# A conformer-style layer on one core: POOL splits the weights of the first pass, ScalarE forms scale and shift

## What is computed

```python
cs = jax.nn.silu(c)
mod = cs @ ada_w[i] + ada_b[i]
sh1, sc1, g1, sh2, sc2, g2 = [m[:, None, :] for m in jnp.split(mod, 6, axis=-1)]
h = rms_norm(x, norm1_g[i]) * (1 + sc1) + sh1
y = conformer_conv(h, ...)          # h @ w_in, GLU, causal depthwise conv of 31 taps, LayerNorm, silu, @ w_out
x = x + g1 * y
h = rms_norm(x, norm2_g[i]) * (1 + sc2) + sh2
x = x + g2 * sq_relu_mlp(h, mlp_w1[i], mlp_w2[i])
return rms_norm(x, final_g)
```

## Time and profile before

| | |
|---|---|
| median of 3 runs | 2047.59 us (2047.4 to 2048.08) |
| profiled execution | 2046.6 us, span 2044.8 us, granted clock 0.987 |
| TensorE busy | 1983.2 us (97%) |
| VectorE busy | 1073.0 us (52%) |
| ScalarE busy | 669.7 us (33%) |
| POOL busy | 322.8 us (16%) |
| first matmul of the first pass, last of its two joined chunks | 37.07 us, 149.10 us |

### The profile page before, as it was taken

How to read it: one execution, slowest core, us unless ns; L and a number is a source line. 1 busy time by engine, 2 the same in 40 slices (tenths; PEclk the granted TensorE clock), 3 DMA queues, 4 the chain that set the end, 5 groups by cost and what they waited for, 6 DMA issues and landing times.

```text
span 2044.8 us, 21628 instructions
## 1 busy us (share of the span) xinstructions
PE 1983.2 (97%) x8658; PEld 1622.4 (79%) x8658; DVE 1073.0 (52%) x1158; ACT 669.7 (33%) x715; POOL 322.8 (16%) x193
## 2 busy tenths in 40 slices
PE   6889999999999999999999999999999999999996
PEld 3668888868787888888888888888888888888885
DVE  5979999978797877233223323333332332233244
ACT  4335555444333331321231132133123213212333
POOL 3639999920000000000000000000000000000001
PEclk9999999989999999999999999999999999999998
DMA  9962222246796567222222222222222222222212
GB/s 397 399 239 95 91 103 103 83 174 236 303 407 235 211 256 293 83 102 103 90 95 103 97 88 103 103 83 102 103 87 98 103 103 82 103 103 83 101 62 82
DMA packets 46083, 300.72 MB, mean 147 GB/s; under 512 B 4704, under 2 KB 4704, under 8 KB 10976
## 3 DMA queue, kind: packets, MB, share of 16 engines
q1 hardware_dynamic: 46048, 300.29, 39.1%
HBM read 296.08 MB, written 4.19 MB: 147 GB/s over the span
## 4 chain that ended last, share of the span: by engine, by line
PE 89%; DVE 8%; ACT 1%; DMA 1%; issue 1%; SPq 0%; DVEq 0%; ACTq 0%
PE ps L396 58%; PE ps L401 29%; DVE adar L912 2%; DVE raw L912 2%; DVE wlo L929 1%; DVE hlo L918 1%; PE ps L475 1%; DMA adar<-ada 1%; PE ps L509 0%; DMA xb<-xT 0%; DVE quad L925 0%; DVE xb L1227 0%; PE ps L467 0%; ACT hhi L760 0%; ACT whi L616 0%
## 5 line engine op out<-in xcount | busy, mean ns | idle before, releaser
L396 PE MATMUL ps<-hlo,whi 128*128 128x512 f32 (+1 forms) x1792 | 653.9, 392 | 13.2 <-DVE hlo L918 13.2
L396 PE MATMUL ps<-hhi,whi 128*128 128x512 f32 (+1 forms) x1792 | 653.2, 391 | 11.1 <-ACT sig L774 4.8
L616 ACT ACTIVATE whi<-raw 128x2048 fp32r<-128x2048 f32 x176 | 336.4, 1911 | 656.2 <-PE ps L401 656.2
L401 PE MATMUL ps<-hhi,wlo 128*128 128x512 f32 (+1 forms) x1792 | 437.2, 390 | 0.0
L929 DVE TENSOR_TENSOR wlo<-raw,whi 128x2048 fp32r<-128x2048 f32 x151 | 346.0, 2291 | 120.2 <-ACT whi L616 120.2
L396 PEld LDWEIGHTS ps<-hlo,whi 128*128 128x128 f32 x1792 | 337.1, 189 | 87.6 <-issue 11.4
L396 PEld LDWEIGHTS ps<-hhi,whi 128*128 128x128 f32 x1792 | 338.3, 189 | 83.7 <-issue 7.9
L396 PE MATMUL ps<-dhi,whi 128*128 128x512 f32 x1024 | 397.0, 389 | 0.0
L396 PE MATMUL ps<-dlo,whi 128*128 128x512 f32 x1024 | 397.0, 389 | 0.0
L401 PEld LDWEIGHTS ps<-hhi,wlo 128*128 128x128 f32 x1792 | 338.0, 189 | 70.6
L1160 DVE SCALAR_TENSOR_TENSOR xb<-ps,modb,xb 128x512 f32<-128x512 f32 x128 | 90.4, 747 | 363.1 <-PE ps L401 353.3
(11 more groups left out here) (122 smaller groups left out, 828.6 us busy)
## 6 DMA issues: line engine op xcount, KB each, us to landing
raw<-w SPq DMA_DIRECT2D x176, 1024.0 KB, 4.8
raw<-ada SPq DMA_DIRECT2D x56, 1024.0 KB, 7.4
adar<-ada SPq DMA_DIRECT2D x40, 1024.0 KB, 7.2
xb<-xT SPq DMA_DIRECT2D x8, 1024.0 KB, 8.8
out<-xb SPq DMA_DIRECT2D x5, 512.0 KB, 4.2
out<-xb SPq DMA_DIRECT2D x6, 256.0 KB, 3.7
csb<-c SPq DMA_DIRECT2D x1, 1024.0 KB, 4.7
quad<-c SPq DMA_DIRECT2D x1, 1024.0 KB, 7.0
```

The source lines that it names most:

```text
L396: return pe.matmul(ps[:, bank, :], whi[:, slot, tile * P:(tile + 1) * P], x, start=first, stop=False, skip_group_check=True)
L401: return pe.matmul(ps[:, bank, :], wlo[:, slot, tile * P:(tile + 1) * P], x, start=False, stop=last, skip_group_check=True)
L616: act.activation(whi[:, q % WS, :], raw_slot(q), ACT.Copy).then_inc(whi_done, 1)
```

## The change

1. POOL splits weight units 0 to 9 in the order in which they come (before, VectorE split 0 to 8 and POOL began with 9). `raw_slot(q)` gives it the right slot.
2. POOL's 48 one-column operations and their semaphore go. VectorE multiplies the scale's bias with `norm1_g` once, for all chunks (one more small step, `small` ends one higher), and ScalarE forms scale and shift of chunk k itself, in two one-column activations ahead of `h_first(k)`.
3. VectorE does ada units 0 and 1 before it waits for the parameters.
4. VectorE's order for chunk k is: ada unit 2k + 2, `scale_x(k + 1)`, `lo_part(k)`, ada unit 2k + 3 (chunks 0 and 1 differ: 4 and 5, and none).
5. ScalarE's `split_hi((k + 1) / 2)` stands behind `h_first(k)` instead of ahead of it.
6. In the first pass TensorE does chunk 14 for all banks ahead, without waiting for the low part of chunk 15; only chunk 15 is done bank by bank.

```diff
@@ -53,7 +53,7 @@
 GLU_AT = {1: (4, 6), 2: (5, 14), 3: (6, 22), 5: (7, 3), 6: (8, 10), 7: (9, 16), 8: (10, 22), 10: (11, 8),
           11: (12, 15), 12: (13, 20)}
 FIN_POOL = 11
-SMALL_G1 = 2 * KC + 4
+SMALL_G1 = 2 * KC + 5
 
 
 PARAMS = [("ada_b", ADA), ("norm1_g", KC), ("norm2_g", KC), ("final_g", KC), ("b_in", 2 * KC), ("b_dw", KC),
@@ -419,7 +418,7 @@
                         last = low(o, s, 8 * kk + o, ch(hhi, k), False)
                 last.then_inc(unit_done, 1)
 
-            def outer_units(q, h0, order=range(8)):
+            def outer_units(q, h0, order=range(8), chunk_first=False):
                 for s in range(2):
                     outer_unit(q, s, h0)
                 with loop(ET.PE, 1, 3) as i:
@@ -427,9 +426,19 @@
                         outer_unit(q, s, h0, i)
                 outer_unit(q, 0, h0, 3)
                 pe.wait_ge(wlo_done, q + 8)
+                kks = (0, 1)
+                if chunk_first:
+                    pe.wait_ge(hhi_done, h0 + KC - 1)
+                    for o in range(8):
+                        high(o, 1, o, ch(hhi, KC - 2), False)
+                    pe.wait_ge(hlo_done, h0 + KC - 1)
+                    for o in range(8):
+                        high(o, 1, o, ch(hlo, KC - 2), False)
+                        low(o, 1, o, ch(hhi, KC - 2), False)
+                    kks = (1,)
                 pe.wait_ge(hlo_done, h0 + KC)
                 for n, o in enumerate(order):
-                    for kk in range(2):
+                    for kk in kks:
                         k = KC - 2 + kk
                         high(o, 1, 8 * kk + o, ch(hhi, k), False)
                         high(o, 1, 8 * kk + o, ch(hlo, k), False)
@@ -486,7 +495,7 @@
 
             keep_busy(14, 0, 1)
             pe.wait_ge(rstd_done, 1)
-            outer_units(A0, 0)
+            outer_units(A0, 0, chunk_first=True)
 
             for s in range(2):
                 pe.wait_ge(glu_done, s + 1)
@@ -649,9 +658,17 @@
             root(1, 7)
             preload(ACT.Sigmoid)
 
+            def scale_shift(k):
+
+                act.wait_ge(ada_used, 2 * k + 2)
+                act.activation(modb[:, 2 * k:2 * k + 1], mod[:, 2 * k:2 * k + 1], ACT.Identity,
+                               scale=col("norm1_g", k), bias=b1p[:, k:k + 1]).then_inc(small, 1)
+                act.activation(modb[:, 2 * k + 1:2 * k + 2], mod[:, 2 * k + 1:2 * k + 2], ACT.Identity,
+                               bias=col("ada_b", 2 * k + 1)).then_inc(small, 1)
+
             def h_first(k):
 
-                act.wait_ge(small, 2 * k + 4)
+                act.wait_ge(small, 2 * k + 5)
                 act.wait_ge(scaled_done, k + 1)
                 if k >= 2:
                     act.wait_ge(hlo_done, k - 1)
@@ -659,13 +676,13 @@
                                bias=modb[:, 2 * k + 1:2 * k + 2]).then_inc(hf_ready, 1)
                 h_hi(k, k, h32[k % 2])
 
-            h_first(0)
-            for k in range(1, KC):
+            act.wait_ge(par_in, 16)
+            act.wait_ge(small, 3)
+            for k in range(KC):
+                scale_shift(k)
+                h_first(k)
                 if k % 2:
                     split_hi((k + 1) // 2)
-                h_first(k)
-
-            act.wait_ge(par_in, 16)
 
             def sigmoid(c, bank, n):
 
@@ -896,10 +913,6 @@
                 dve.wait_ge(dv, steps[0])
 
             dve.memset(ones[:], 1.0).then_inc(ones_set, 1)
-            dve.wait_ge(par_in, 16)
-            dve.tensor_scalar(b1p[:, 0:KC], pr[:, COL["ada_b"]:COL["ada_b"] + 2 * KC:2], 1.0, None, ALU.add
-                              ).then_inc(small, 1)
-            dve.tensor_scalar(b1p[:, KC:2 * KC], col("ada_b", M_SC2, KC), 1.0, None, ALU.add).then_inc(small, 1)
 
             def variance(bank):
                 chain(dve.tensor_scalar(st[:, 0:4], ps[:, bank, 0:4], 1.0 / D, EPS, ALU.mult, ALU.add))
@@ -938,26 +951,31 @@
                     dve.tensor_tensor(ssum[:], ssum[:], src[:], ALU.add).then_inc(done, 1)
 
             dve.wait_ge(cs_ready, 1)
-            for a in range(3):
-                ada_reduce(a)
+            ada_reduce(0)
+            ada_reduce(1)
+            dve.wait_ge(par_in, 16)
+            dve.tensor_scalar(b1p[:, 0:KC], pr[:, COL["ada_b"]:COL["ada_b"] + 2 * KC:2], 1.0, None, ALU.add
+                              ).then_inc(small, 1)
+            dve.tensor_scalar(b1p[:, KC:2 * KC], col("ada_b", M_SC2, KC), 1.0, None, ALU.add).then_inc(small, 1)
+            dve.wait_ge(small, 2)
+            dve.tensor_tensor(b1p[:, 0:KC], b1p[:, 0:KC], col("norm1_g", 0, KC), ALU.mult).then_inc(small, 1)
+            ada_reduce(2)
             dve.wait_ge(stat_done, 1)
             variance(5)
             ada_reduce(3)
-            split_lo(0)
             dve.wait_ge(rstd_done, 1)
             scale_x(0)
             for k in range(KC):
-                if k < KC - 2:
-                    ada_reduce(2 * k + 4)
+                a = (4, ADA0, 6)[k] if k < 3 else 2 * k + 2
+                if a < ADA0:
+                    ada_reduce(a)
                 if k < KC - 1:
                     scale_x(k + 1)
-                if k < KC - 2:
-                    ada_reduce(2 * k + 5)
                 lo_part(k, k, h32[k % 2])
-                if k % 2:
-                    split_lo((k + 1) // 2)
+                if a < ADA0:
+                    ada_reduce(a + 1)
             dve.wait_ge(hlo_done, KC)
-            n_small = 2 + 2 * KC
+            n_small = 3 + 2 * KC
 
             def glu(c, bank):
 
@@ -1231,7 +1249,7 @@
         def _(pool):
             def split_lo(q, off=0):
                 pool.wait_ge(whi_done, q + 1 + off)
-                pool.tensor_tensor(wlo[:, q % WS, :], raw[:, q % RAW, :], f(whi[:, q % WS, :]), ALU.subtract
+                pool.tensor_tensor(wlo[:, q % WS, :], raw_slot(q), f(whi[:, q % WS, :]), ALU.subtract
                                    ).then_inc(wlo_done, 1)
 
             def c_sums(c):
@@ -1249,18 +1267,9 @@
                                pattern=[[-1, P]], channel_multiplier=1).then_inc(ident_set, 1)
             pool.memset(s1[:], 0.0).then_inc(s1_done, 1)
             pool.memset(s2[:], 0.0).then_inc(s2_done, 1)
-            pool.wait_ge(small, 2)
-            for k in range(KC):
-                pool.wait_ge(ada_used, 2 * k + 2)
-                pool.tensor_tensor(modb[:, 2 * k:2 * k + 1], mod[:, 2 * k:2 * k + 1], b1p[:, k:k + 1], ALU.add
-                                   ).then_inc(mod_sum, 1)
-                pool.tensor_tensor(modb[:, 2 * k + 1:2 * k + 2], mod[:, 2 * k + 1:2 * k + 2],
-                                   col("ada_b", 2 * k + 1), ALU.add).then_inc(small, 1)
-                pool.wait_ge(mod_sum, k + 1)
-                pool.tensor_tensor(modb[:, 2 * k:2 * k + 1], modb[:, 2 * k:2 * k + 1], col("norm1_g", k), ALU.mult
-                                   ).then_inc(small, 1)
-            pool.wait_ge(wlo_done, A1 + 1)
-            split_lo(A1 + 1)
+            for q in range(A1 + 2):
+                split_lo(q)
+
             def side_sums(c):
 
                 part, n0 = side_sum[c % 2], adds_until(c)
```

More of the change, by code:

```diff
@@ L149, in trunk_kernel @@
         small = sem("small")
-        mod_sum = sem("mod_sum")
         row_done = sem("row_done")
```

## The result

The changed kernel takes 2054.8 us (median of 6 runs, 2053.32 to 2055.5), the kernel before 2047.49 in the runs beside it: a ratio of 1.0037, with a 95% interval of 1.0027 to 1.0048. The forecast was 2057.1. So the change costs 7.3 us, in the direction and by the mechanism that was forecast, and a little less than the 9.5 expected.

A forecast was written before the change was run, and what follows sets the result against it. VectorE was taken to bound the first pass; later work only shifts. Holds and the last wait gave +17.4, the shorter tail -8.3, the clock +0.9: +10.0, forecast as +9.5 on 2047.59, so 2057.1 us; own range 2053.5 to 2061, 8-in-10 range 2034 to 2062.

The forecast's parts named there:

- the term for the hold: First pass: each of eight POOL splits holds VectorE 4.6 us, from bounds 0 and 4.63; 36.8 us in all.
- the one meeting at 424.66: In the convolution, an ada unit starting under a POOL split's last 0.19 us took 2.33 us for 2.29: 0.04 delay.
- POOL's reads would fill the path throughout: POOL needs 2.17 ns per element, VectorE 1.05, so POOL's two reads would fill one shared read path.
- hlo(15): Last low part of the first pass: to end at 152.8 us against 135.44, +17.4.
- The wait ahead of it: VectorE's wait for the last chunk's high part, ahead of the last low part: 2.1 us for 4.0 before.
- The tail: Behind the last low part TensorE has 24 matmuls, not 48: 5.6 us in place of 13.9, so -8.3.
- the low clock: TensorE's reduced clock at the first pass's end, after gaps: bounds 0 and 2.8 us, taken as 0.9.
- The whole: At the end of the first pass: +17.4 - 8.3 + 0.9 = +10.0 us; forecast as +9.5.
- Edits costed at nothing: First pass: two ada units ahead of the parameters, and low part behind one ada unit, each to change nothing.
- the cover of 0.7 us: First pass: h needs 2.1 us after its ada unit, its low part follows after 2.8; 0.7 us is left.
- not held: Rival: POOL's splits don't hold VectorE, transfers bound the first pass at 12.3 us a period; -22 us, 2025.5; chance 0.18.
- Shared at half pace: Rival: VectorE runs at half pace during POOL's splits, losing 2.2 us each; -9.5 us, 2038; chance 0.12.

The follow-up runs named there:

- the third experiment: Changed kernel with VectorE splitting units 0 to 7 again, plus ScalarE's high split ahead of scale and shift, unit 8's low split on VectorE: 2046.15 us.
- the fill: Changed kernel with POOL's splits of units 0 to 7 replaced by zero fills of the same tile, reading nothing from SBUF: 2026.34 us, ratio 0.99.
- the pieces: Changed kernel with each of POOL's splits of units 0 to 7 done as four instructions of 512 columns: 2055.61 us, ratio 1.0042.

## Why the prediction was right, and where its terms were off

*The direction* came from the term for the hold, taken at its upper end, 4.6 us. It is 4.41 for seven splits (the 6.69 us instructions) and 4.14 for the first, which holds a small step (4.82 for 0.68). Eight holds cost 35.0 us where the sum had 36.8. The text had named 4.45 as the other value; that one was nearly exact. The row that decided it, the one meeting at 424.66, showed the very end of a hold, and it said more than I took from it: that ada unit ends 2.14 us behind POOL's split (426.99 for 424.85), as the held one of the timeline above does (67.02 for 64.87, 2.15). The operation that waits out an ada unit showed the same exclusion from the other side. That POOL's reads would fill the path throughout, which I worked out from the time per element, was not tested by itself.

*hlo(15)* was to end at 152.8 and ended at 151.56: the holds took 1.8 less, and the statistic on which ada unit 3 waits came 0.4 later in this execution (30.66 for 30.27). The wait ahead of it, 2.1 in the sum, was 2.15; ScalarE's two new steps lie 0.3 apart for the 0.2 that I took from rows 11, which the margin in that sum covered.

*The tail* was to take 5.6 us and took 5.62. The 0.9 us that stood for the low clock was not needed: the clock was at 1.00 from 131 to 160 us. It fell in the middle instead (0.88 from 50 to 120), where VectorE is the bound, and cost nothing. I had placed the risk at the wrong end, and had judged it by the length of the gap ahead, which doesn't decide it alone: eight matmuls took 3.75 us behind gaps of 3.34 and 3.58 us and 3.65 behind one of 1.94, but 2.12 behind one of 2.82.

*The whole*: at the first matmul behind the pass the sum gave +10.0 and the trace has +7.9: 1.8 too much for the holds and 0.9 for the clock, 0.4 too little for the start, and 0.2 of rounding. The medians moved by 7.3.

*Edits costed at nothing*: the two ada units ahead of the parameters ran in idle time (8.18 and 16.34 us), and what follows still waited for the statistic, 3.25 us, as forecast. Of the cover of 0.7 us for the low part behind one ada unit I only said that it is left; the third experiment shows how thin it is: any delay on ScalarE's queue is on the path. That ScalarE's split behind h keeps it whole is worth 8.6 us in the new order, all of it ahead of the last chunk, where the prediction saw 1.9 at the last chunk. This was an error that by luck didn't show, since both halves of the change came together.

*The rivals*: not held (2025.5, 22 us below the kernel before) has its size about confirmed by the fill, 2026.34, 20.8 below. Shared at half pace is excluded by the ada units of 6.69 us, where it asked for 4.4, and by the pieces, which are served one after the other. Its terms, 1.9 and 8.3 less 0.9, add up to 9.3 and not to the 9.5 of the text, which changes nothing.

## What to carry to other kernels

Where VectorE is the bound and its instructions have two SBUF inputs, elementwise work that POOL does in its place, reading SBUF, costs VectorE nearly POOL's whole duration, here 4.41 us to save 2.20. It was not so against VectorE instructions with one SBUF input, nor where POOL only wrote. A held instruction is booked as busy, so compare durations of the same form, not waits. And cost a bundle edit by edit: here the other edits, good together (9.3 us), were hidden under one bad one (17.2), and the kernel with only the good ones is the one to keep.

## What the runs showed of the hardware that was not expected

- Between POOL and VectorE neither is starved: POOL's four pieces and VectorE's instructions alternate strictly. They go in the order in which they were issued: VectorE has each next instruction issued some 0.08 us before the end of the last (94.65 for 94.72), but POOL's next piece is there before it (92.53). POOL's split, issued under an ada unit, lost 1.5 us in this way (6.09 us for the 4.63 of rows 8).
- POOL's fill of 128x2048 takes 1.81 us, less than four times the 0.52 of 512 columns.
- VectorE's row sum with one input takes 2.27 us, the product with a row sum 2.28: the second input costs nothing but the exposure.
